# Rotate-half moved from matmuls to ScalarE copies, and four re-orderings around the mixer of a two-layer decoder trunk

## The reference, cut to what matters

```python
def rope(a, pos, inv_freq):
    ang = pos.astype(jnp.float32)[:, :, None, None] * inv_freq
    cos, sin = jnp.cos(ang), jnp.sin(ang)
    a1, a2 = jnp.split(a.astype(jnp.float32), 2, axis=-1)
    return jnp.concatenate([a1 * cos - a2 * sin, a2 * cos + a1 * sin], axis=-1).astype(a.dtype)

    for l in range(DEPTH):
        h = rmsnorm(x, ln_mix[l])
        (hq, hf, hi, hg, rq, rk, rv, rg, sq, sk, sv, gate_logits) = jnp.split(h @ w_in[l], IN_SPLITS, axis=-1)
        f_gate = lb + (1.0 - lb) * jax.nn.sigmoid(z)          # z = hf
        k_in = (1.0 - lb) * jax.nn.sigmoid(-z)
        oa = hgrn2_chunkwise(qa, k_in, hi, log_f)             # then norm, silu(hg), w_br_hgrn
        ob = retention_chunkwise(rope(rq), rope(rk), rv, ...) # then norm, silu(rg), w_br_ret
        oc = swa_sink_attention(rope(sq), rope(sk), sv, ...)  # then w_br_swa
        mixed = gates[:, :, 0] * y_a + gates[:, :, 1] * y_b + gates[:, :, 2] * y_c
        x = x + mixed @ w_out[l]
        x = x + memory_cross_attention(rmsnorm(x, ln_xq[l]), rmsnorm(mem, ln_xkv[l]), ...)
        x = x + peer_ffn(rmsnorm(x, ln_ffn[l]), ...)
```

## Time and profile before

| what | value |
|---|---|
| median of 3 runs | 2420.35 us (2418.95 to 2420.59) |
| the profiled execution | 2419.26 us, its span 2417.5 us |
| granted clock of TensorE, mean over the span | 0.999 |
| busy: PE, DVE, ACT, POOL | 99%, 68%, 55%, 45% |
| instructions | 43,862 |

### The profile page before, as it was taken

How to read it: one execution, slowest core, us unless ns; L and a number is a source line. 1 busy time by engine, 2 the same in 40 slices (tenths; PEclk the granted TensorE clock), 3 DMA queues, 4 the chain that set the end, 5 groups by cost and what they waited for, 6 DMA issues and landing times.

```text
span 2417.5 us, 43862 instructions
## 1 busy us (share of the span) xinstructions
PE 2385.2 (99%) x15876; PEld 2168.0 (90%) x15876; DVE 1646.6 (68%) x3223; ACT 1318.2 (55%) x2048; POOL 1097.3 (45%) x452
## 2 busy tenths in 40 slices
PE   9999999999999999999999999999999999999999
PEld 8999888999999888888889898889999998888887
DVE  7467634879995556777664686258799946667776
ACT  5575555565555555554555655555555545555444
POOL 5776777787773000000067767767877730000000
PEclk9999999999999999999999999999999999999999
DMA  7544555456767667777654445544567776667775
GB/s 240 169 140 140 172 170 164 158 182 216 241 241 253 208 207 225 245 244 245 206 190 155 148 140 173 176 157 157 182 218 242 255 231 205 213 225 238 245 246 169
DMA packets 186554, 485.37 MB, mean 201 GB/s; under 512 B 14272, under 2 KB 81088, under 8 KB 181824
## 3 DMA queue, kind: packets, MB, share of 16 engines
q1 hardware_dynamic: 179808, 443.26, 55.4%
q10 hardware_dynamic: 6624, 40.44, 4.9%
HBM read 449.04 MB, written 34.60 MB: 200 GB/s over the span
## 4 chain that ended last, share of the span: by engine, by line
PE 89%; DVE 8%; ACT 2%; issue 1%; DMA 0%; SPq 0%; DVEq 0%
PE banks L894 29%; PE banks L493 13%; PE banks L495 13%; PE banks L494 13%; PE banks L836 5%; PE banks L522 5%; PE banks L865 3%; PE banks L837 3%; PE banks L523 2%; DVE arena L1692 1%; DVE arena L1738 1%; DVE arena L1690 1%; PE banks L797 1%; PE banks L781 1%; PE banks L762 1%
## 5 line engine op out<-in xcount | busy, mean ns | idle before, releaser
L423 POOL TENSOR_TENSOR w_lo<-ring,w_hi 128x1024 fp32r<-128x1024 f32 x448 | 1097.1, 2457 | 861.9 <-ACT w_hi L925 861.1
L925 ACT ACTIVATE w_hi<-ring 128x1024 fp32r<-128x1024 f32 x776 | 818.8, 1056 | 431.5 <-PE banks L894 338.6
L493 PE MATMUL banks<-h_r,w_hi 128*128 128x256 f32 x2464 | 702.5, 285 | 6.8 <-ACT arena L1000 5.6
L495 PE MATMUL banks<-h_r,w_lo 128*128 128x256 f32 x2464 | 697.0, 283 | 0.0
L494 PE MATMUL banks<-h_r,w_hi 128*128 128x256 f32 x2464 | 696.9, 283 | 0.0
L894 PE MATMUL banks<-w_hi,o_r 128*128 128x512 f32 x2048 | 559.8, 390 | 0.0
L493 PEld LDWEIGHTS banks<-h_r,w_hi 128*128 128x128 f32 x2464 | 472.0, 192 | 10.6 <-issue 8.8
L494 PEld LDWEIGHTS banks<-h_r,w_hi 128*128 128x128 f32 x2464 | 472.2, 192 | 0.6 <-issue 0.5
L495 PEld LDWEIGHTS banks<-h_r,w_lo 128*128 128x128 f32 x2464 | 472.1, 192 | 0.0
L894 PEld LDWEIGHTS banks<-w_hi,o_r 128*128 128x128 f32 x2048 | 380.0, 188 | 79.4
L1945 DVE TENSOR_TENSOR w_lo<-ring,w_hi 128x1024 fp32r<-128x1024 f32 x320 | 390.0, 1219 | 31.4 <-ACT w_hi L925 31.4
(11 more groups left out here) (303 smaller groups left out, 3219.6 us busy)
## 6 DMA issues: line engine op xcount, KB each, us to landing
ring<-in_stream SPq DMA_DIRECT2D x776, 512.0 KB, 3.3
gates_dram<-o_f ACTq DMA_DIRECT2D x32, 1024.0 KB, 5.5
o_f<-gates_dram SPq DMA_DIRECT2D x32, 1024.0 KB, 7.2
arena<-in_mem ACTq DMA_DIRECT2D x2, 1024.0 KB, 10.3
arena<-in_keys ACTq DMA_DIRECT2D x2, 1024.0 KB, 7.0
arena<-in_c_decay ACTq DMA_DIRECT2D x2, 768.0 KB, 5.0
x<-in_x SPq DMA_DIRECT2D x4, 256.0 KB, 5.8
out_dram<-arena SPq DMA_DIRECT2D x4, 256.0 KB, 2.1
```

Source lines behind the costliest of these rows:

```text
L423: pool.tensor_tensor(w_lo[:, s, :], ring[:, s, :], w_hi[:, s, :], ALU.subtract).then_inc(sem(f"low{s}"), 1)
L493: pe.matmul(out, lhs[0], rhs[0], start=first, stop=False)
L495: return pe.matmul(out, lhs[1], rhs[0], start=False, stop=last)
L925: act.activation(w_hi[:, s, :], ring[:, s, :], ACT.Copy).then_inc(sem(f"high{s}"), 1)
```

## The change

1. The rotated halves are made by ACT: `Copy` with scale 1 or -1 from SBUF into the PSUM banks where the matmuls wrote, by two halves of 64 partitions for the retention and four quarters of 32 partitions for the window, the window's as soon as two SQ tiles are out. The matmuls, the constant and its DMA go.
2. The window's second half, the HG evacuations, the sigmoids, the gate tiles and `level_exp` get another order on ACT; HI's results are copied out before three weight tiles are rounded. HGRN operands 1 and 2 are made before the first scores are taken, in other SBUF regions.
3. Memory's norm and scaling go to the retention and to the window's rope, half before and half after it.
4. The first two OUT tiles are interleaved on PE, and the loop over OUT is written out.

```diff
-                for n, src in enumerate((rq, rk)):
-                    for j in range(2):
-                        m = pe.matmul(bank[:, 2 * n + j, :], rot[:, 0, :], src[:, 2 * j:2 * j + 2, :],
-                                      start=True, stop=True)
...
+                def rotate(dst, src, dim, done, halves=None):
+                    half = dim // 2
+                    for p0 in range(0, P, half) if halves is None else halves:
+                        first = p0 % dim == 0
+                        p1 = p0 + half if first else p0 - half
+                        act.activation(dst[p0:p0 + half], src[p1:p1 + half], ACT.Copy, scale=-1.0 if first else 1.0
+                                       ).then_inc(sem(done), 1)
...
+                for s in range(SLOTS):
+                    evac(G_SQ, s, wqk[:, s:s + 1, :])
+                    if s == 1:
+                        ev("ret_decayed")
+                    if s % 2:
+                        copied(T_SQ + s + 1)
+                        rotate(turned[:, s - 1:s + 1, :], wqk[:, s - 1:s + 1, :], SWA_DIM, "win_rotated")
...
+                if l == 0:
+                    pe.wait_ge(sem("angles"), 4)
+                    rms_sums(square, KC, sem("mem_squared"), 1, bank[:, 6, 0:T]).then_inc(sem("mem_summed"), 1)
...
-                for n, (dst, src, scale) in enumerate(((cum, hf, 1.0), (kin, hf, -1.0), (qin, hq, 1.0))):
...
+                evac(G_HG, 0, hg[:, 0:1, :])
+                gate_sigmoid(cum, hf, 1.0)
+                gate_sigmoid(kin, hf, -1.0)
+                evac(G_HG, 1, hg[:, 1:2, :])
+                gate_sigmoid(qin, hq, 1.0)
                 window_turned(0)
...
+                gate_out(0)
+                ev("forget")
+                act.activation(cum, cum, ACT.Ln).then_inc(sem("log_forget"), 1)
+                gate_out(1)
+                window_exp(1, (0, 1))
+                gate_out(2)
+                window_exp(1, (2, 3))
+                gate_out(3)
+                level_exp(1)
...
+                window_softmax(1, first_span)
+                level_operands(1)
+                level_operands(2)
+                window_low(1)
+                link(take_level(0))
+                for i in range(3, 9):
+                    link(take_level(i - 2))
+                    level_operands(i)
...
+                    link(dve.reciprocal(minv[:, :], minv[:, :]))
...
+                scaled_mem(range(KC // 2))
                 out_of_banks(T_HF)
...
+                scaled_mem(range(KC // 2, KC))
                 ev("ret_rooted")
...
+                def wide_two(g, n, src, pairs):
+                    for s, chunks in ((0, (0, 1, 2, 3, 4, 5)), (1, (0, 1, 2, 3)), (0, (6, 7)), (1, (4, 5, 6, 7))):
```

More of the change, by code:

```diff
@@ L120, in lay_constants @@
     return {
-        "c_freq": freq, "c_rot": rot, "c_decay": decay.astype(f), "c_level": level, "c_window": window,
+        "c_freq": freq, "c_decay": decay.astype(f), "c_level": level, "c_window": window,
         "c_ident": np.eye(P, dtype=f), "c_iota": np.broadcast_to(np.arange(P, dtype=f), (P, P)).copy(),
@@ L220, in build @@
         qin = part(13056, 4 * T)
-        left = part(0, 4 * T)
-        right = part(1024, 4 * T)
-        operands = ((left, right), (part(7680, 4 * T), part(8704, 4 * T)))
+        operands = ((part(11776, 4 * T), part(6656, 4 * T)), (part(7680, 4 * T), part(8704, 4 * T)))
         span = part(2048, 4 * T)
@@ L599, in _ @@
                 ev("ret_decayed")
+                if l == 0:
+                    pe.wait_ge(sem("mem_rooted"), 1)
                 weighted(rv, retained, 6).then_inc(sem("ret_summed"), 1)
                 all_free(T_HF)
[L603 to L606, removed]
                 for t in range(NT):
@@ L703, in level_across @@
                     ev("level_ready", 9, 9)
+                    lt, rt = operands[0]
                     for hd in range(HEADS):
-                        m = pe.matmul(bank[:, 2, hd * P:(hd + 1) * P], left[:, hd * T:hd * T + P],
-                                      right[:, hd * T + P:(hd + 1) * T], start=True, stop=True)
+                        m = pe.matmul(bank[:, 2, hd * P:(hd + 1) * P], lt[:, hd * T:hd * T + P],
+                                      rt[:, hd * T + P:(hd + 1) * T], start=True, stop=True)
                     m.then_inc(sem("level_scored"), 1)
@@ L743, in _ @@
                 settle()
-                with pe.Fori(0, 2) as i:
-                    for s in range(SLOTS):
-                        wide_tile(G_OUT + i, s, T_OUT + i * SLOTS + s, h_r, pairs=None if s else "mixed_low")
+                wide_two(G_OUT, T_OUT, h_r, "mixed_low")
+                for s in (2, 3):
+                    wide_tile(G_OUT, s, T_OUT + s, h_r)
+                group(G_OUT + 1, T_OUT + SLOTS, wide_tile, h_r)
                 ev("mn_low", KC, KC)
@@ L1735, in _ @@
                 link(dve.tensor_tensor(summed, summed, hgs, ALU.mult))
-                ev("mem_loaded", 16, 16)
-                for k in range(KC):
-                    dve.scalar_tensor_tensor(mem[:, k, :], mem[:, k, :], gain["xkv"][:, k:k + 1], minv[:, :],
-                                             ALU.mult, ALU.mult).then_inc(sem("mn_made"), 1)
                 ev("hgrn_rooted")
```

127 lines of the change are left out of this document (66 added, 61 removed).

## The result

The changed kernel takes 2437.37 us (median of four runs, 2434.28 to 2442.59) beside 2420.24 of the kernel before: a ratio of 1.0074, 95% interval 1.0056 to 1.0092, or 17.1 us slower. I had forecast 2412.0, in a range up to 2417, with a chance of 0.04 for slower.

The account below looks back on a forecast made before the run. PE, busy 2385.2 of 2417.5 us, was taken as the bound. 11.2 - 1.4 - 6.4 + 4.0 + 1.0 = 8.4 off the profiled 2419.26 gave 2411.0, as a median 2412; range 2399 to 2417.

Parts of the forecast that it names:

- Rotations, gain 11.2: Rotation products of retention and window leave PE: 3.43 and 2.15 us in each of two layers, 11.2 gained.
- rival C: Slower kernel: copies of a quarter of the partitions cost more than whole ones, before the HF roundings; some 2426 us, chance 0.03.
- HI, HG and gates, loss 6.4: ACT's new order starts DVE's chain 3.0 later; PE waits 3.3 and 3.1 a layer, 12.8, less 6.4 that goes.
- forget chain: DVE's twelve instructions up to `forget`, held by POOL at the gates: 16 to 17 us, with instructions of 2.4 or more.
- rival A: The forget chain is not held by POOL: 2396.5 us if fully free, about 2402 with `forget` 11.7 after the sigmoids; chance 0.32.
- Levels, gain 4.0 with bounds of 1.7 and 5.3: PE's waits for HGRN operands, 2.65 us a layer, shrink to 0.65 at the last level: gain 2 x 2.0.
- OUT, gain 0: The 0.70 wait before the first tile's fifth chunk stays; interleaving only moves the fourth pair of low halves.
- Memory and angles, 1.4 lost and 1.0 gained: First layer: PE waits for DVE's angles before memory sums, 1.4 lost; earlier scaling takes 0.5 off BR1's wait per layer.
- BR1's wait: PE's wait for BR1's gated sum: loses 0.5 in each layer by earlier memory scaling, expected at 0.4.

## Why the prediction was wrong

**Rotations, gain 11.2: right.** Measured 12.3 alone. No wait came at HF, and rival C's copies cost what whole ones do.

**HI, HG and gates, loss 6.4: right in size, by luck.** 6.2 alone. The forget chain took 15.9 (136.13 to 152.02) with four instructions held to 2.3 to 3.3, where I had said 16 to 17, so rival A fell. But the sum was not made of what I had put in. With the gates alone PE's waits grew by 2.4, and most of the 6.2 is the clock, which I had not counted (two falls in the profile, up to 5.1). The gates' waits in the changed kernel were 2.79, 1.59, 2.67 and 2.92, 10.0 in all, and not 3.3 and 3.1 in each layer, 12.8 in all; and with ACT's old order they are 10.4, so what the new order costs there is the cover of the first layer, which the memory's move takes in any case.

**Levels, gain 4.0 with bounds of 1.7 and 5.3: the step that failed most, 16 off.** "ACT makes each exponential one to two tiles earlier, so every even level has slack of 1 to 8 us by my count" reckoned an early place in an in-order queue as early work. The exponential isn't done earlier, since DVE's span isn't there; what is done later is all that stands behind it. The levels cost 12.1 alone; moving three exponentials back gave all of it back.

**OUT, gain 0: the second step that failed.** "It only moves the fourth pair, and that did not make PE wait" looked at PE's own data alone. The earlier trace rows stayed at 0.70 as I said, but I didn't ask whose slots and banks now come free together. 8.5 to 10.4.

**Memory and angles, 1.4 lost and 1.0 gained.** BR1's wait fell to 0.49, as forecast from the earlier trace rows; the angles cost 2.4 to 3.6 rather than 1.4. The sentence "the memory sums themselves only move" is the error here: they were 3.6 us of cover for ACT and DVE ahead of the gates. I had reckoned with that in the gates' waits ("The layers are now alike"), but not seen that it belongs to this part and is paid without the new gate order too: 11.8 alone, 6.2 on top of gates and levels, 4 when it is undone in the changed kernel.

**The clock: no term at all.** I priced every wait at its length. About 10 of the 15 us of the span are what came behind waits.

The runs lie on one path from the kernel before to the changed one: rotations -12.3 (2407.73), then gates and levels +14.8 (2422.55), memory +6.2 (2428.71, the run with OUT undone), OUT +8.7 (2437.37), together 17.3. My terms in the same order were -11.2, +2.4, +0.4 and 0. So I was off by 12.4 on gates and levels, 5.8 on the memory's move and 8.7 on OUT, and by 1.1 the other way on the rotations.

## What to carry to other kernels

An instruction placed earlier in an in-order queue than its input is ready delays all that stands behind it; look at what stands behind before counting slack. Where two engines lock each other out, look for the pauses of the one that has the work: a change that lets two of its inputs go together takes the pause away, and the other engine waits out whole instructions. A wait of PE of 2 to 3 us is here better priced at its length and 1.7 more, while PE work ahead of a tight place can be free. And undoing one part of a change shows nothing of its cost where another part has already spoiled the same place.

## What the runs showed of the hardware that was not expected

PE's clock falls behind short waits, but not behind each, and it is a good part of what the waits cost. Over the 18 profiles, in the mixers, OUT and the start of the second layer, 62 of 75 waits of 2.0 us or more were followed by a stretch with a mean granted clock under 0.8 in the 4 us behind them, and 6 of 40 waits of 1.2 to 2.0; 36 more of 1.5 in the later stages were followed by none. Of these 68 falls 55 last 3.4 us and 13 last 6.8, which costs up to twice 1.7. The same wait of 2.91 at the same tile of the second layer, with rotations alone and then with the memory's move added:

```profile
1344.50:1348.50 4.00, 4.00 (x32) 3.87 (x33) 1.39 (x4) 4.00 (x13) 2.45 (x2) 1.00 0.00 1
```

```profile
1355.10:1359.10 4.00, 3.98 (x21) 4.00 (x22) 1.39 (x4) 3.88 (x12) 2.42 (x2) 0.57 0.02 6
```

32 products start in one and 21 in the other, with the other engines about equally busy. That PE stands still is a condition at the two places of OUT that were filled with products; what decides between equal waits no run here settles. The Trainium skill (TensorE: Matmul & The Clock Gate, "The HAM clock gate") has the clock set by how busy PE has been recently. That the fall went when PE was kept busy agrees with it; two equal waits with unlike outcomes are not explained by that alone.
